# An FFN in three parts, and the modulation weights multiplied inside the first three FFNs

## What is computed

```python
mx = (silu(c) @ mod_w[i] + mod_b[i]).reshape(bsz, 9, 1, 1024)      # mod_w: 2 x 1024 x 9216
mc = (silu(c_ctx) @ mod_w[i] + mod_b[i]).reshape(9, 1, 1, 1024)
x = x + 0.5 * mx[:, 2] * swiglu(ada_norm(x, g, mx[:, 0], mx[:, 1]), w13, w2)   # inner width 2816
hx = ada_norm(x, g1, mx[:, 3], mx[:, 4]);  x = x + mx[:, 5] * mixer(hx, hc)
x = x + 0.5 * mx[:, 8] * swiglu(ada_norm(x, g2, mx[:, 6], mx[:, 7]), w13b, w2b)
```

## Time and profile before

| | us |
|---|---|
| median of 3 runs | 2680.08 |
| lowest, highest | 2679.24, 2689.0 |
| span of the profiled execution | 2684.1 |
| PE busy | 2475.2 (92%) |
| VectorE busy | 1302.4 (49%) |
| ScalarE busy | 828.1 (31%) |
| POOL busy | 723.5 (27%) |

### The profile page before, as it was taken

One profiled execution on the slowest core, in us unless ns is written; L12 is line 12 of the kernel. 1 busy time (PEld: TensorE's weight loads), 2 busy tenths in 40 slices (PEclk: granted clock), 3 DMA queues, 4 the chain that ended last, 5 costly groups with the idle time before them and its releaser, 6 DMA issues.

```text
span 2684.1 us, 36549 instructions
## 1 busy us (share of the span) xinstructions
PE 2475.2 (92%) x13638; PEld 2003.6 (75%) x13638; DVE 1302.4 (49%) x1688; ACT 828.1 (31%) x973; POOL 723.5 (27%) x605
## 2 busy tenths in 40 slices
PE   8979989999959988999998999997799999987997
PEld 3445558888849976888886888886788888877997
DVE  7675553333333235333335333333777777754445
ACT  1011133332220033333224333223333343323553
POOL 2088731111223312111131111120333333322111
PEclk9989989999955588999999999996899999987999
DMA  8878842222386421222222222221000000002543
GB/s 310 310 265 304 312 158 94 94 89 87 105 215 194 128 90 63 94 94 95 89 94 81 96 99 93 86 96 51 32 31 31 31 31 31 31 1 88 174 163 123
DMA packets 76343, 312.31 MB, mean 116 GB/s; under 512 B 24960, under 2 KB 34560, under 8 KB 47744
## 3 DMA queue, kind: packets, MB, share of 16 engines
q1 hardware_dynamic: 61808, 282.52, 31.3%
q0 software_dynamic: 4256, 25.10, 2.3%
q10 hardware_dynamic: 10224, 3.94, 0.7%
HBM read 281.19 MB, written 30.34 MB: 116 GB/s over the span
## 4 chain that ended last, share of the span: by engine, by line
PE 64%; issue 15%; DVE 8%; POOL 6%; DMA 3%; ACT 2%; SPq 1%; DVEq 1%; ACTq 0%; POOLq 0%
PE PS L173 16%; PE PS L174 16%; PE PS L175 16%; PE PS L450 5%; PE PS L867 4%; POOL EE L1561 2%; DVE t L600 2%; DVE wlo L193 2%; ACT whi L189 1%; POOL DTs L1551 1%; PE PS L863 1%; DVE v L600 1%; PE PS L441 1%; POOL X L1557 1%; PE PS L848 1%
## 5 line engine op out<-in xcount | busy, mean ns | idle before, releaser
L173 PE MATMUL PS<-hh,whi 128*128 128x512 f32 (+1 forms) x1792 | 664.5, 371 | 49.4 <-DVE hl L316 38.3
L174 PE MATMUL PS<-hl,whi 128*128 128x512 f32 (+1 forms) x1792 | 655.9, 366 | 0.0
L175 PE MATMUL PS<-hh,wlo 128*128 128x512 f32 (+1 forms) x1792 | 652.2, 364 | 0.0
L193 DVE TENSOR_TENSOR wlo<-raw,whi 128x2048 fp32r<-128x2048 f32 x180 | 456.1, 2534 | 381.8 <-ACT whi L189 381.8
L189 ACT ACTIVATE whi<-raw 128x2048 fp32r<-128x2048 f32 x180 | 344.4, 1913 | 321.0 <-PE PS L175 314.1
L173 PEld LDWEIGHTS PS<-hh,whi 128*128 128x128 f32 x1792 | 341.2, 190 | 127.6 <-issue 44.6
L175 PEld LDWEIGHTS PS<-hh,wlo 128*128 128x128 f32 x1792 | 341.8, 191 | 57.3
L174 PEld LDWEIGHTS PS<-hl,whi 128*128 128x128 f32 x1792 | 342.3, 191 | 50.4
L450 PE MATMUL PS<-modw,cvec 128*2 128x256 f32 x1152 | 262.4, 383 | 11.3 <-DMA modw<-in_mod_w 11.1
L173 PE MATMUL PS<-hidh,whi 128*128 128x512 f32 (+1 forms) x704 | 257.4, 366 | 5.5 <-DVE wlo L193 5.5
L429 POOL CAST hidh<-gt 128x512 f32 (+1 forms) x88 | 49.0, 557 | 781.2 <-DVE gt L388 781.2
(11 more groups left out here) (270 smaller groups left out, 3190.7 us busy)
## 6 DMA issues: line engine op xcount, KB each, us to landing
modw<-in_mod_w SPq DMA_DIRECT2D x72, 1024.0 KB, 5.0
raw<-in_w_f0a SPq DMA_DIRECT2D x22, 1024.0 KB, 4.8
raw<-in_w_f1a SPq DMA_DIRECT2D x22, 1024.0 KB, 4.8
raw<-in_w_f2a SPq DMA_DIRECT2D x22, 1024.0 KB, 4.9
raw<-in_w_f3a SPq DMA_DIRECT2D x22, 1024.0 KB, 4.8
raw<-in_w_gdn SPq DMA_DIRECT2D x16, 1024.0 KB, 4.8
raw<-in_w_f0b SPq DMA_DIRECT2D x16, 704.0 KB, 4.0
raw<-in_w_f1b SPq DMA_DIRECT2D x16, 704.0 KB, 4.0
```

What stands on the lines that cost most here:

```text
L173: pe.matmul(dst, w_h, xh, start=first, stop=False)
L174: pe.matmul(dst, w_h, xl, start=False, stop=False)
L175: return pe.matmul(dst, w_l, xh, start=False, stop=last)
L193: dve.tensor_tensor(wlo[:, s, :], raw[:, s, :], whi[:, s, :].bitcast(F32), ALU.subtract)\
```

## The change

FFNs are cut into three parts of 8, 8 and 6 inner tiles. Each part has its own up phase (as many blocks as tiles) and down phase of 4 blocks; a down block holds two output tiles over the part's inner tiles, and each part adds its share to x, so that x is updated 24 times in an FFN instead of 8. hidh and hidl shrink to 8 tiles, and the room is taken by two slots of modulation weights.

The weights are cut into 9 groups of two vectors (2048 columns), each in 8 steps, one for each 128 rows of mod_w, 1 MB a step. A step (`mods_step`) is four fp32 matmuls of 512 columns into the four 32-partition quarters of one PSUM bank, each with a column tile of its own and with cvec repeated to 32 columns as weights. The first group runs ahead of the S5 rounds. The other eight run in the first eight FFN parts, a step behind each block; the parts of 6 tiles have their last two steps behind the first two down blocks. Behind the first output tile of the part's down phase (the third block's in parts of 6) PE turns the rows (`mods_turn`), and VectorE adds the bias (`mods_take`). SP's queue issues a step's load behind each raw load. The loops of these eight parts are written out. The norm and the gates wait for the group that holds their vectors.

```diff
-FH = FT // 2
+PARTS = [(0, 8), (8, 16), (16, FT)]
...
+def ffn_phases(f):
+    return [one for p, (t0, t1) in enumerate(PARTS)
+            for one in ((f"f{f}p{p}a", t1 - t0, BLK), (f"f{f}p{p}b", KT // 2, 2 * (t1 - t0) * P))]
...
+MS = 2
+MG = 2 * NMOD * KT // 16
+MODS_IN = {(0, 0): 1, (0, 1): 2, (0, 2): 3, (1, 0): 4, (1, 1): 5, (1, 2): 6, (2, 0): 7, (2, 1): 8}
...
-        hidh = sb("hidh", [P, FT, T], F32R, ffn)
-        hidl = sb("hidl", [P, FT, T], F32R, ffn)
+        hidh = sb("hidh", [P, PARTS[0][1], T], F32R, ffn)
+        hidl = sb("hidl", [P, PARTS[0][1], T], F32R, ffn)
+        modw = sb("modw", [P, MS, 4 * 512], F32, ffn)
...
+            for p, (t0, t1) in enumerate(PARTS):
+                a, b, n = f"f{f}p{p}a", f"f{f}p{p}b", t1 - t0
+                g, hosts = mods_after(f, p)
+                pairs = FT // 2 * f + t0 // 2
+                def up(i):
+                    for s in range(2):
+                        pe.wait_ge(wlo_ready[s], 1 + BASE[a] // 2 + i + 1)
+                        pe.wait_ge(gt_ready[s], 1 + pairs + i)
+                        for ab in range(2):
+                            for k in range(KT):
+                                if p == 0 and s == 0 and ab == 0:
+                                    pe.wait_ge(norm_done, made + len(halves(c0)) * (k + 1))
+                                last = mm3(pe, PS[:, 2 * ab + s, c0:T], s, (2 * k + ab) * P, hh[:, k, c0:T], hl[:, k, c0:T],
+                                           k == 0, k == KT - 1)
+                        last.then_inc(blk_done[s], 1)
+                        if g:
+                            mods_step(pe, g, 2 * i + s, 7)
+                def down(i):
+                    for s in range(2):
+                        pe.wait_ge(wlo_ready[s], 1 + BASE[b] // 2 + i + 1)
+                        for q in range(2):
+                            pe.wait_ge(x_ready[q], 1 + X_BEFORE[stage] + KT // 2 * p + 2 * i + s)
+                            for k in range(n):
+                                if s == 0 and q == 0 and k >= n - 2:
+                                    pe.wait_ge(hid_ready[k % 2], 1 + pairs + n // 2)
+                                last = mm3(pe, PS[:, 4 + q, c0:T], s, (n * q + k) * P, hidh[:, k, c0:T], hidl[:, k, c0:T],
+                                           k == 0, k == n - 1)
+                            if q == 0:
+                                last.then_inc(acc_even, 1)
+                                if g and 2 * i + s == (0 if hosts == KT else 2):
+                                    mods_turn(pe, g)
+                            else:
+                                last.then_inc(blk_done[s], 1)
+                        if g and hosts + 2 * i + s < KT:
+                            mods_step(pe, g, hosts + 2 * i + s, 7)
+                loop(pe, n // 2, g, up)
                 for s in range(2):
-                    pe.wait_ge(wlo_ready[s], 1 + BASE[a] // 2 + i + 1)
-                    pe.wait_ge(gt_ready[s], 1 + FT // 2 * f + i)
-                    for ab in range(2):
-                        for k in range(KT):
-                            if s == 0 and ab == 0:
-                                pe.wait_ge(norm_done, made + len(halves(c0)) * (k + 1))
-                            last = mm3(pe, PS[:, 2 * ab + s, c0:T], s, (2 * k + ab) * P, hh[:, k, c0:T], hl[:, k, c0:T],
...
+                def update(i, s):
+                    if g and (i, s) == ((0, 0) if hosts == KT else (1, 0)):
+                        mods_take(dve, g)
+                        if p == 0:
+                            dve.wait_ge(mods_ready, mods_done(layer, n_, 2))
+                    dve.wait_ge(acc_even, KT // 2 * (len(PARTS) * f + p) + 2 * i + s + 1)
+                    add_to_x(dve, layer, n_, 4 * i + 2 * s, c0, 4, None).then_inc(x_ready[0], 1)
+                    dve.wait_ge(blk_done[s], 1 + BASE[b] // 2 + i + 1)
+                    add_to_x(dve, layer, n_, 4 * i + 2 * s + 1, c0, 5, None).then_inc(x_ready[1], 1)
...
+        def mods_step(pe, g, k, bank):
+            if k == 0 and g:
+                pe.wait_ge(mod_rows, g)
+            pe.wait_ge(mod_in[k % MS], 16 * ((KT * g + k) // MS + 1))
+            for j in range(4):
+                last = pe.matmul(PS[32 * j:32 * j + 32, bank, :], cvec[:, k, :], modw[:, k % MS, 512 * j:512 * j + 512],
+                                 start=k == 0, stop=k == KT - 1, tile_position=(0, 32 * j))
+            last.then_inc(mod_used[k % MS], 1)
+        def mods_rows(act, g, bank):
+            act.wait_ge(mod_used[MS - 1], 1 + KT // MS * (g + 1))
+            act.wait_ge(mod_turned, g)
+            act.activation(rows[:, :], PS[:, bank, :], ACT.Copy).then_inc(mod_rows, 1)
+        def mods_turn(pe, g):
+            pe.wait_ge(mod_rows, g + 1)
+            if g:
+                pe.wait_ge(mods_ready, MODS_DONE[g - 1])
+            pick = const("eye").rearrange("p (j r) -> p j r", j=4)[:, :, 0:2]
+            for t in range(4):
+                dst = PS[:, 6, 0:32].rearrange("p (j t w) -> p j t w", j=4, w=2)[:, :, t, :]
+                last = pe.matmul(dst, rows[:, t * P:(t + 1) * P], pick, start=True, stop=True)
+            last.then_inc(mod_turned, 1)
+        def mods_take(dve, g):
+            vector = mods[:, :, :, :].rearrange("p l a w -> p (l a) w")[:, 16 * g:16 * g + 16, :]
+            bias = modb[:, :, :].rearrange("p l a -> p (l a)")[:, 16 * g:16 * g + 16]
+            dve.wait_ge(mod_turned, g + 1)
+            dve.tensor_tensor(vector, PS[:, 6, 0:32].rearrange("p (a w) -> p a w", w=2),
+                              bias.unsqueeze(2).to_broadcast([P, 16, 2]), ALU.add).then_inc(mods_ready, 1)
+            dve.wait_ge(mods_ready, (MODS_DONE[g - 1] if g else 1) + 1)
+            for h_ in range(2):
+                layer, n, kind = vector_kind(2 * g + h_)
+                one = vector[:, KT * h_:KT * h_ + KT, :]
+                if kind == 1:
+                    dve.scalar_tensor_tensor(out=gs[:, layer, n, :, :], in0=one, scalar=1.0,
                                              in1=ng[:, layer, n, :].unsqueeze(2).to_broadcast([P, KT, 2]),
-                                             op0=ALU.add, op1=ALU.mult)
-                    last = dve.tensor_scalar(hg[:, layer, n, :, :], gate, 1.0 if n == 1 else 0.5, None, ALU.mult)
-            last.then_inc(mods_ready, 1)
+                                             op0=ALU.add, op1=ALU.mult).then_inc(mods_ready, 1)
+                elif kind == 2:
...
-            mods_act(act, 0, MHEAD)
+            mods_rows(act, 0, 4)
...
-            mods_pe(pe, 0, MHEAD)
+            pe.wait_ge(silu_c, 1)
+            for k in range(KT):
+                mods_step(pe, 0, k, 4)
+            mods_turn(pe, 0)
...
+            def load_mods(g, k):
+                sp.wait_ge(mod_used[k % MS], 1 + KT // MS * g + k // MS)
+                sp.dma_start(modw[:, k % MS, :], A["mod_w"][KT * g + k]).then_inc(mod_in[k % MS], 16)
+            def load_both(name, g, k0, end):
+                for j in range(COUNT[name]):
+                    s = j % 2
+                    sp.wait_ge(wlo_ready[s], 1 + (BASE[name] + j) // 2)
+                    sp.dma_start(raw[:, s, 0:COLS[name]], A["w_" + name][j]).then_inc(raw_in[s], 16)
+                    if k0 + j < end:
+                        load_mods(g, k0 + j)
...
+            load_mods(0, 0)
+            load_mods(0, 1)
...
+            for k in range(MS, KT):
+                load_mods(0, k)
...
+                elif name[0] == "f" and mods_after(int(name[1]), int(name[3]))[0]:
+                    g, hosts = mods_after(int(name[1]), int(name[3]))
+                    load_both(name, g, 0 if name[4] == "a" else hosts, hosts if name[4] == "a" else KT)
...
-         "cvec": np.stack([tiles(I["c_ctx"]), tiles(I["c"][0])], axis=-1),
+         "cvec": np.tile(np.stack([tiles(I["c_ctx"]), tiles(I["c"][0])], axis=-1), (1, 1, 16)),
```

More of the change, by code:

```diff
@@ L75 @@
 X_STAGE_OF_FFN = [0, 2, 3, 5]
+X_UPDATES = [len(PARTS) * KT // 2 if k == "ffn" else KT // 2 for _, _, _, k in NORMS]
+X_BEFORE = [sum(X_UPDATES[:m]) for m in range(len(NORMS) + 1)]
 SUM_STEPS = 1 + 2 * (KT - 2)
@@ L121, in program @@
         gwal = sb("gwal", [P, KT, 4 * H], F32R)
-        cvec = sb("cvec", [P, KT, 2])
+        cvec = sb("cvec", [P, KT, 32])
         PS = ctx.enter_context(nc.psum_tensor("PS", [P, 8, 512], F32))
@@ L194, in split_lo, with blocks, one @@
                 .then_inc(wlo_ready[s], 1)
-        def blocks(eng, name, split, work, start=0):
+        def blocks(eng, name, split, work, written_out=None):
             n, u0 = COUNT[name] // 2, BASE[name] // 2
             whole = n - (BASE[name] + COUNT[name] == BLOCKS)
-            with eng.Fori(0, whole) as i:
+            def one(i):
                 split(eng, 1, u0 + i)
@@ L205, in blocks @@
                 work(i, 1)
+            loop(eng, whole, written_out, one)
             if whole < n:
@@ L340, in final_dve, with loop, mods_after @@
```

(66 more changed lines are left out.)

155 lines of the change are left out of this document (48 added, 107 removed).

## The result

The changed kernel takes **2749.05 us** (median of 4 runs, 2745.01 to 2756.47), the kernel before 2684.54 (4 runs, 2679.24 to 2694.27): a ratio of 1.0229 (95% interval 1.0204 to 1.0253), 2.3% slower. The prediction was 2754.5, in a range of 2715 to 2795. The profiled spans are 2747.2 and 2684.1 us, so +63.1 us where +74.5 was forecast.

The account below looks back on a forecast made before the run. PE bounds the FFNs; in the preparation POOL is about one microsecond a cycle behind PE. Preparation -12, steps +81, turns +8.5, three parts +2, f3 -5 sum to +74.5 on the median 2680.08: 2754.5 us, range 2715 to 2795.

Parts of the forecast that it names:

- The start: Preparation: one more 1 MB weight tile and cvec ahead of the small S5 inputs delay VectorE's setup, 3.8 us later.
- The store of et: Preparation: with less weight traffic beside it, VectorE's wait for this store falls from 21.05 to 11 us, 10 us won.
- The rounds: Preparation: POOL's seven cycles shorten from 28.5 to 27.7 us with PE's modulation gone and less traffic, 5.5 us won.
- The step: FFNs: four column tiles at once 0.86 us plus two changes of form of 0.2; 1.26 us each, 64 steps +81 us.
- The turns: FFNs: PE transposes the modulation rows once in each of 8 parts, 1.06 us a turn, +8.5 us.
- Three parts: Full-width FFNs: more changes from up to down and less time for the norm's sums on POOL, together +2 us.
- FFN 3: Half-width FFN, down phase: blocks of 8 tiles no longer wait for the weight split, 70 us falls to 65, -5 us.
- The waits of the sync queue and the cover of silu: FFNs: later-issued weight loads still land in time, and the last tile's silu chain stays mostly hidden; about no cost.
- pairs only: Rival, FFN steps: only two column tiles overlap, 55 us more, 2810 us; chance 0.10 for pairs or worse.
- late weights: Rival, FFNs: the sync queue's added wait makes raw blocks late by 1 us in 64 blocks, 2818 us; chance 0.05.
- the preparation that collapses: Rival, preparation: waits due to PE and weight traffic vanish, about 65 us go, 2670 us, not slower; chance 0.05.
- the preparation gives nothing: Rival, preparation: store and cycles stay unchanged, 0 instead of -12 us, 2766 us; counted within the forecast.

Follow-up runs that it names:

- the three removals: Kernel before with one of eight matmuls per modulation tile (2699.17 us); kernel before with half of POOL's cx work (2687.49); changed kernel with that half (2714.12).
- the step experiments: Changed kernel with the four matmuls of 56 FFN steps in one column tile (2888.51 us), in two in turn (2800.14), or left out (2682.84).
- thin PE: Kernel before with only one of the eight matmuls of each modulation tile kept, all transfers and waits staying: 2699.17 us.
- the fillers: Changed kernel with 72 fp32 matmuls of constants, results unused, on PE behind seven of the eight S5 rounds: 2743.0 us.
- the spread version: Changed kernel without FFN steps; all 72 steps in the preparation, 36 ahead of the S5 rounds, 5 or 6 behind each of seven: 2676.77 us.
- the kernel before with its 64 bytes: Kernel before with cvec moved behind the FFN's tiles, so hidh, hidl, hh and hl begin 64 bytes lower: 2677.39 us, ratio 0.9952.

## Why the prediction was right, step by step

- **What bounds.** Right: POOL next behind PE by less than a microsecond, and the FFNs with nothing to hide a step. Both were read from the earlier trace rows; the three removals show the first, and the step experiments the second.
- **The start**, +3.8: measured +3.2 (17.27 against 14.07). **The store of et**, 11 us: measured 10.84. **POOL's first operation**, 6 us earlier: 7.1.
- **The rounds**, seven by 0.8 shorter: measured 0. This is the step that failed, and the largest error of the sum (5 us) but for the pace below. Two things were wrong in it. "They end before that landing" was said of the S5 steps on an idle PE. They don't: zs begins only when POOL's cx is ready, that is with the store's issue, and takes 2.5 to 4.5 us in the eight rounds, where the kernel before has 2.46 in all but the first (the turn ahead of it 3.5 to 3.7 instead of 1.97); the store of cx takes 4.63 to 6.85 where the chain shows it. What POOL waited for in the rounds, before and after (us in total, times, longest):

```profile
POOL zd L753 <- DVEq L706: 15.5, 8, 3.0
```

```profile
POOL zd L825 <- DVEq L778: 21.9, 8, 3.9
```

It waits for the landing of cx 3.2 us instead of 8.1, and for zs 6.4 longer (3.7 of them it waited before for the turned bx, just ahead); four of the seven rounds start with zs and not with the landing. From issue to next start it is 5.5 us, where the 27.7 have 5.0 in them and the kernel before has 5.8. The other thing is POOL's own work. From start to issue it is 23.0 us on average, where the forecast had 22.7, as in the kernel before. One operation of POOL takes longer while VectorE works, here of one form, beside VectorE and, in the same round, without it:

```profile
189.48 1.50 POOL L817 TENSOR_TENSOR t<-cf,pw 128x576 f32<-128x576 f32 x1
...
200.85 1.17 POOL L817 TENSOR_TENSOR t<-cf,pw 128x576 f32<-128x576 f32 x1
```

In the last seven rounds 79 of POOL's 98 operations overlap with VectorE's after the change, 69 before it: ten by 0.33 us are 3.3, and POOL's operations add up to 2.4 us more in these rounds. VectorE's tables now fall more on POOL's work than before; that the idle PE shifted them is likely, but not shown (with thin PE in the kernel before, POOL's stretch was 22.8 us, between the two). The two parts, 0.47 and 0.34 us a round, are the 0.8. The rounds of the fillers with zs at full clock, 27.96 us, fit this.
- **The step**, 1.26 us: measured 1.22 between neighbouring blocks, 1.19 by taking the matmuls away. 0.86 for four tiles at once was right; the two changes of form are some 0.35 together instead of 0.4. The estimate by Part 3 of the Trainium skill's page "TensorE: Matmul & The Clock Gate" was 1.49; the measurement speaks against carrying its share for three column tiles over to four.
- **The turns**, 8.5: measured 8 by 0.91, 7.3.
- **Three parts** in FFNs 0 to 2, +2: the spread version, which has the parts and no steps, against the kernel before with its 64 bytes, gives -0.3, +0.9 and +2.6, so +3.2. **FFN 3**, -5: measured -3.9. What PE waited for in it, before and after (us in total, times, longest):

```profile
PE PS L173 <- DVE wlo L193: 9.2, 18, 0.8
```

```profile
PE PS L199 <- DVE wlo L219: 1.1, 3, 0.4
```

The waits went as forecast, 8 us of them. Some 1.5 to 3 came back as a slower pace, which the 64 bytes bring to 256 columns (0.118 to 0.120 us); the 1 to 2.5 us that are still missing to 3.9 are open.
- **The waits of the sync queue and the cover of silu**: at nothing, right. In FFNs 0 to 2 of the changed kernel PE waits for no weights, neither modw nor wlo.
- **Not foreseen**: the pace, about -10 us in FFNs 0 to 2, and -3.3 in the DeltaNet, of which -1.9 came with the 64 bytes alone (it takes 643.3 to 646.1 us in the traces with the new places, 646.3 to 646.7 with the old).

The sum by measured terms: -7.2 + 78 + 7.3 + 3.2 - 10.4 (4752 matmuls by 0.0022, from start to start) - 3.9, and -2.6 for the three other stages, is +64.4; the spans say +63.1. The forecast was 11 us over because an effect that its profile could not show took 10 off; the failed term of the rounds (+5.5) and the smaller steps and turns (-4) nearly cancelled, which is luck. The time lies well inside the range without it. Two slips of the prediction did not matter: its likeliest case ends at 2782 by its own terms, not 2785, and the 402 us that it named for FFNs 0 and 1 leave out the norm ahead of them; the growth that it gave, 33 us, is to be held against 29.5 and 28.7. Of the rivals, pairs only and late weights are refuted, and so is the preparation that collapses: with half of POOL's work gone too it ends at 320 us, and even that kernel (2714.12) is slower than before. That the preparation gives nothing is refuted for the time before the rounds (7.1 us won) and true of the rounds.

## What to carry to other kernels

Before work is moved off the busiest engine, see how long the second chain beside it is, and shorten the two together: here each alone gave at most 0.1 us a round, both 4.5. A chain is not fixed, either: work taken off one engine can lower its clock for the steps that stay, and shift which engines run side by side; here either took a part of the 0.8 us a round that was expected. Work that was hidden should not go where an engine has no idle time; the same steps, placed in the preparation at the rate at which their weights arrive, cost 84 us less in the FFNs and 12 more ahead of them. When an edit moves buffers, compare the pace of one unchanged inner loop before crediting the edit.

## What the runs showed of the hardware that was not expected

- A matmul of 512 fp32r columns starts every 0.2264 us instead of 0.2287 when the activations lie 64 bytes lower in memory (by my reckoning on a multiple of 128 bytes instead of 64 beyond one); with 256 columns it is the other way round, 0.120 against 0.118. Shown by moving one region by 64 bytes and nothing else; the reason is open.
- Four fp32 matmuls in four column tiles cost no more than one (0.86 us and the edges), and getting in and out of them some 0.35 us at full clock.
- Most POOL operations on 128x576 fp32 elements take 0.33 us longer beside VectorE's fp32 operations than without them: 1.17 and 1.50, 1.40 and 1.73, 1.65 and 1.97 us, in the traces before and after alike. Only the first of the seven forms mostly stays at 1.2 us.
- The store of et, 3.15 MB, took 10.84, 21.05 and 26.83 us as the weight loads beside it moved 0, 233 and 303 GB/s.
- The stage of S5 and GLU takes 307 to 312 us in eight of the traces and 315 to 318 in five, with no edit in common. Of the kernel before and of the one with its 64 bytes moved, 310 and 318 us from the stage's start (columns as in the earlier trace rows):

```profile
740.00:1050.00 310.00, 271.82 (x1544) 238.62 (x1543) 102.17 (x120) 58.27 (x67) 88.52 (x62) 0.68 0.52 149
```

```profile
738.00:1056.00 318.00, 278.39 (x1542) 245.16 (x1541) 101.81 (x120) 58.30 (x67) 88.49 (x62) 0.65 0.51 146
```

The same work in the same number of records but two, with 6.6 us more of PE at a lower granted clock. There is one trace for each kernel; that one kernel does both is made likely by the nine runs of the version with all groups in the preparation, six at 2699.7 to 2701.6 us and three, the profiled one among them, at 2707.9 to 2710.1. No edit here explains it, and a single profile can be off by 8 us for this alone; so the verdicts above on small differences go by stages or by the intervals.
